# First block, w_o: merged tiles split during the last branch, running sums of the norm behind the last product

## The reference, cut to what matters

```
merged = (gates[:, :, 0] * (y_a @ w_branch[0])
          + gates[:, :, 1] * (y_b @ w_branch[1])
          + gates[:, :, 2] * (y_c @ w_branch[2]))
mix = merged @ w_o
x = layer_norm(ALPHA * x + mix, ln1_g, ln1_b)      # mean and variance over the 1024 features
ffn = conv_ffn(x, w_up, conv_w, conv_b, w_down)
```

## Time and profile before

| | us |
|---|---|
| median of 3 runs | 3969.03 (3965.19 to 3970.46) |
| the profiled execution's own time | 3969.89 |
| its span | 3968.1 |
| PE busy | 3705.0 (93%) |
| DVE busy | 1700.1 (43%) |
| ACT busy | 1516.1 (38%) |
| POOL busy | 1311.7 (33%) |

### The profile page before, as it was taken

The page is one execution under the profiler, slowest core; times in us unless marked ns, Lnnn a source line. Parts: engine busy times, 40 slices in busy tenths (PEclk is TensorE's granted clock), DMA queues, the critical chain, the costliest instruction groups (busy, mean ns, idle before and its releaser), DMA issues.

```text
span 3968.1 us, 47959 instructions
## 1 busy us (share of the span) xinstructions
PE 3705.0 (93%) x17594; PEld 2921.5 (74%) x17594; DVE 1700.1 (43%) x2434; ACT 1516.1 (38%) x2470; POOL 1311.7 (33%) x600
## 2 busy tenths in 40 slices
PE   8989997999898999989998799999899898999998
PEld 7777785888687777768887576888534687777886
DVE  3444346543334433664325642503447443425042
ACT  3246632432322665233324544423243233444232
POOL 4422132444343112334443243344201011443442
PEclk9989998999998999999999899999999999999999
DMA  3211121322222111222332132222123100322222
GB/s 136 98 67 43 43 75 57 102 95 101 88 92 96 43 43 49 90 69 95 101 101 91 64 104 77 85 99 97 65 69 91 33 1 1 101 96 81 100 95 80
DMA packets 100066, 308.85 MB, mean 78 GB/s; under 512 B 25920, under 2 KB 26048, under 8 KB 99520
## 3 DMA queue, kind: packets, MB, share of 16 engines
q1 hardware_dynamic: 81792, 298.90, 22.4%
q10 hardware_dynamic: 18112, 7.68, 0.8%
HBM read 301.30 MB, written 4.19 MB: 77 GB/s over the span
## 4 chain that ended last, share of the span: by engine, by line
issue 45%; PE 35%; POOL 16%; DVE 2%; ACT 1%; DVEq 0%; POOLq 0%; DMA 0%; SPq 0%; ACTq 0%
POOL ring_r L2584 16%; PE ps L437 8%; PE ps L438 8%; PE ps L439 8%; PE ps L915 2%; PE ps L1015 1%; PE ps L934 1%; PE ps L596 1%; PE ps L1083 0%; PE ps L1060 0%; PE ps L1091 0%; PE ps L1073 0%; PE ps L1051 0%; PE ps L1093 0%; PE ps L1153 0%
## 5 line engine op out<-in xcount | busy, mean ns | idle before, releaser
L2584 POOL TENSOR_TENSOR ring_r<-ring,rounded_r 128x1024 fp32r<-128x1024 f32 x520 | 1272.6, 2450 | 2156.7 <-ACT rounded_r L1196 2156.2
L437 PE MATMUL ps<-source_hi,rounded_r 128*128 128x512 f32 x2560 | 1019.7, 398 | 120.4 <-DVE X_lo L1886 30.9
L1196 ACT ACTIVATE rounded_r<-ring 128x1024 fp32r<-128x1024 f32 x520 | 550.4, 1059 | 1383.1 <-PE ps L439 1214.0
L438 PE MATMUL ps<-source_hi,ring_r 128*128 128x512 f32 x2560 | 1007.2, 393 | 0.0
L437 PEld LDWEIGHTS ps<-source_hi,rounded_r 128*128 128x128 f32 x2560 | 487.7, 191 | 238.0 <-DVE N_lo L2181 33.4
L439 PE MATMUL ps<-X_lo,rounded_r 128*128 128x512 f32 x1536 | 602.5, 392 | 0.0
L438 PEld LDWEIGHTS ps<-source_hi,ring_r 128*128 128x128 f32 x2560 | 487.8, 191 | 101.9 <-issue 2.6
L439 PEld LDWEIGHTS ps<-X_lo,rounded_r 128*128 128x128 f32 x1536 | 291.0, 189 | 61.6
L439 PE MATMUL ps<-N_lo,rounded_r 128*128 128x512 f32 x768 | 303.0, 394 | 0.0
L2141 DVE SCALAR_TENSOR_TENSOR T<-ps,PAR,T 128x511 f32<-128x511 f32 (+1 forms) x176 | 131.5, 749 | 229.4 <-ACT T L1384 214.5
L437 PE MATMUL ps<-H_hi,rounded_r 128*128 128x512 f32 x512 | 199.2, 389 | 0.0
(11 more groups left out here) (496 smaller groups left out, 5791.6 us busy)
## 6 DMA issues: line engine op xcount, KB each, us to landing
ring<-in_weights SPq DMA_DIRECT2D x560, 512.0 KB, 3.3
X<-in_x SPq DMA_DIRECT2D x2, 1024.0 KB, 7.0
out_x<-X SPq DMA_DIRECT2D x4, 512.0 KB, 2.6
SWAP<-Z ACTq DMA_DIRECT2D x4, 256.0 KB, 3.3
MEM<-in_mem ACTq DMA_DIRECT2D x1, 1024.0 KB, 4.7
diag_in<-Y ACTq DMA_DIRECT2D x8, 128.0 KB, 2.2
Z<-diag_in ACTq DMA_DIRECT2D x8, 128.0 KB
diag_out<-Z ACTq DMA_DIRECT2D x2, 512.0 KB, 4.4
```

The source lines that it names most:

```text
L437: mm(o, lh, rh, start=start, stop=False)
L438: mm(o, ll, rh, start=False, stop=False)
L1196: av(RH[:, j, :], ring[:, j, :], ACT.Copy).then_inc(w_hi, 1)
L2584: nc.gpsimd.tensor_tensor(RL[:, j, :], ring[:, j, :], RH[:, j, :].bitcast(F32), ALU.subtract).then_inc(w_lo, 1)
```

## The change

Three edits, in the first block of each layer.

* DVE and ACT: the splits of the merged tiles are put between the work on the last branch. ACT makes `MR[0]`, `MR[1]` behind the round of c = 9, `MR[2]`, `MR[3]` behind c = 10, `MR[4]`, `MR[5]` behind c = 11, then rounds the fourth slot, then makes `MR[6]`, `MR[7]`. DVE makes `ML[0]` to `ML[3]` just ahead of the gate multiplies of tiles 4 to 7, and `ML[4]` to `ML[7]` behind tile 7.
* PE: `first_quad` of w_o takes its first nine steps in a skewed order, (lane 0, k 0), (0, 1), (1, 0), (1, 1), (0, 2), (1, 2), (2, 0), (2, 1), (2, 2), and goes on from k = 3 abreast as before. Each lane now also waits until DVE has read its PSUM bank (`mg`).
* PE: `sums` and `sums_of(6)` stand behind the last product, ahead of `sums_of(7)`; nothing stands ahead of it or inside it.

```diff
+            def first_quad(split, bank, hi, lo, ready, base, step=1, banks_free=None, lanes=RING - 1, before=None, skewed=False):
+                def step_of(k, j):
+                    pe.wait_ge(ready, base + step * (k + 1))
+                    if k == 0:
+                        pe.wait_ge(w_lo, split + (j + 1))
+                        if banks_free is not None:
+                            pe.wait_ge(banks_free[0], banks_free[1] + (j + 1))
+                    ins = three(ps[:, bank + j, :], wh(j, k), wl(j, k), tile(hi, k), tile(lo, k), k == 0, k == KT - 1)
+                    if k == KT - 1:
+                        ins.then_inc(used, 1)
+                if skewed:
+                    for j in range(2):
+                        for k in range(2):
+                            step_of(k, j)
+                    for j in range(2):
+                        step_of(2, j)
+                    for k in range(3):
+                        step_of(k, 2)
+                for k in range(3 if skewed else 0, KT):
...
                     for j in range(lanes):
+                        step_of(k, j)
...
-                first_quad(W0 + n_split(B_WO), 0, MR, ML, y_lo, l * Y_N + 12)
+                first_quad(W0 + n_split(B_WO), 0, MR, ML, y_lo, l * Y_N + 12, 1, (mg, l * 24 + 24), skewed=True)
                 shift(l, 0)
                 for j in range(RING):
                     pe.wait_ge(x1pre, l * RING + RING + (j + 1))
-                    if j == RING - 1:
-                        sums(l, 0)
-                    product(W0 + (n_split(B_WO) + RING + j), j, j, MR, ML, (lambda: sums_of(l, 0, KT - 2)) if j == RING - 1 else None)
+                    product(W0 + (n_split(B_WO) + RING + j), j, j, MR, ML)
+                sums(l, 0)
+                sums_of(l, 0, KT - 2)
                 sums_of(l, 0, KT - 1)
...
+                def merged_high(*tiles):
+                    for n in tiles:
+                        act.wait_ge(mg, l * 24 + 4 + 16 + n + 1)
+                        av(MR[n], M[n], ACT.Copy).then_inc(y_hi, 1)
                 for c in range(12):
                     act.wait_ge(used, C + B_BR + c + 1)
                     ahead(Q + (B_BR + c) // RING, c % RING)
-                for n in range(KT):
-                    act.wait_ge(mg, l * 24 + 4 + 16 + n + 1)
-                    av(MR[n], M[n], ACT.Copy).then_inc(y_hi, 1)
+                    if c >= 9:
+                        merged_high(2 * (c - 9), 2 * (c - 9) + 1)
                 last_slot(Q + B_WO // RING)
+                merged_high(6, 7)
...
+                def merged_low(n):
+                    dve.wait_ge(y_hi, l * Y_N + 12 + n + 1)
+                    remainder(ML[n], M[n], MR[n].bitcast(F32), y_lo)
                 for b in range(3):
                     for n in range(KT):
+                        if b == 2 and n >= 4:
+                            merged_low(n - 4)
...
-                for n in range(KT):
-                    dve.wait_ge(y_hi, l * Y_N + 12 + n + 1)
-                    remainder(ML[n], M[n], MR[n].bitcast(F32), y_lo)
+                for n in range(4, KT):
+                    merged_low(n)
```

More of the change, by code:

```diff
@@ L451, in wl @@
                 return RL[:, j, k * P:k * P + P]
-            def first_quad(split, bank, hi, lo, ready, base, step=1, banks_free=None, lanes=RING - 1, before=None):
-                for k in range(KT):
+            def first_quad(split, bank, hi, lo, ready, base, step=1, banks_free=None, lanes=RING - 1, before=None, skewed=False):
[17 more added lines that the diff above has]
+                for k in range(3 if skewed else 0, KT):
                     if before is not None and k == before[0]:
                         before[1]()
-                    pe.wait_ge(ready, base + step * (k + 1))
                     for j in range(lanes):
[L460 to L466, removed]
+                        step_of(k, j)
                 for j in range(lanes, RING):
```

## The result

The changed kernel takes 3941.11 us (median; 3939.27 to 3945.74, 4 runs) against 3969.57 us: the ratio is 0.9932, 95% interval 0.9915 to 0.9949, so 28.5 us less where 25.6 were forecast. The same kernel, run again later beside some of the experiments, gave 3940.27 against 3970.91 us, ratio 0.9915 (0.9902 to 0.9929). The profiled execution has a span of 3943.9 us.

A forecast was written before the change was run, and what follows sets the result against it. PE, busy 93% of the span, was taken as the bound, so only its gaps or slow-clock stretches could give time: 6.1 + 6.7 = 12.8 us per layer, 25.6 for both, giving 3943.4 us; range 3936 to 3953.

The forecast's parts named there:

- The first gap: PE's wait before w_o for the first low part: 7.5 us per layer, 5.1 idle, the rest at half clock.
- Part 1: Splits of the merged tiles during the last branch, so w_o starts without the gap: gain 6.1 us per layer.
- the wait of 0.8 us at k = 3: At the start of w_o, PE waits 0.8 us for `ML[3]`, taken as held by POOL until 603.1.
- The holds: DVE steps reading two on-chip tiles beside a POOL operation end only behind it; `ML[1]` held to 594.9.
- Part 2: Sums moved behind the last w_o product, so the square of tile 7 comes earlier: gain 6.7 us per layer.
- The wait for weights ahead of the last product: At the end of w_o, PE idles 2.0 us until POOL delivers the last chunk's low part.
- The moved sums are hidden: Behind the last product, four moved products (3.4 us) cost nothing; PE has 1.6 us of slack before the mean.
- The sum: Both gains added over the first block: 12.8 us per layer, 25.6 for both layers.
- the one given 0.12: DVE held less than counted at w_o's start, by `ML[3]` in time or halved rates: 3941 to 3942.5; chance 0.12.
- The reading by which contention halves the rates: DVE and POOL each run at half rate when sharing memory: 14.1 us per layer, 3940.8; chance called small.
- The slow tail: Last w_o product runs at 1.2 GHz throughout, moved sums end late: 9.8 us per layer, 3949.4; chance 0.08.
- hold-and-clock rival: POOL holds DVE more, PE waits some 2 us at w_o's start, clock falls: 10.5 per layer, 3948.0; chance 0.08.

The follow-up runs named there:

- the filled gap: Kernel before the change, with 23 matmuls of unused result between the last branch and w_o in each layer; ratio 1.0004 to before.
- the sums alone: Kernel before the change, with only the sums moved behind the last w_o product; 3957.95 us, ratio 0.9965 to before.
- weights early: Changed kernel, with the last w_o chunk rounded ahead of the square of tile 4 instead of behind it; 3944.95 us in one execution.
- more sums: Changed kernel, with four more full-precision matmuls of unused result between the last product and the moved sums; ratio 0.9921 to before.
- unskewed kernel: Changed kernel, with the first nine w_o steps abreast again, lanes 0, 1, 2 for each k; 3955.38 us, ratio 0.996 to before.

## Why the prediction was right

* *The first gap costs 7.5 us, 5.1 idle and the rest clock.* Right. The twelfth w_o matmul now comes 7.5 us earlier (9.98 to 2.49; 7.3 in layer 1), and the filled gap gives 2.1 of them back with w_o starting no earlier.
* *Part 1, 6.1 us per layer.* The mechanism was right, the size low: 7.0 and 6.9 from the border to DVE's first residual (15.66 against 22.69, 15.61 against 22.52). The term that was mis-sized is the wait of 0.8 us at k = 3, which did not come. (The sum also takes off 0.1 for which it names no row.) I had `ML[3]` lose a race of 0.2 us against POOL, with the transfer of the fourth slot read from coarse slices and ACT's round at 3.3 us behind the border. ACT started it at 3.7, POOL at 4.8, and `ML[3]` had begun at 4.2. Lane 2 was expected 0.5 late and starts 0.36 late (603.62 instead of 603.26).
* *The holds.* `ML[1]` was expected to end at 594.9, 4.3 us behind the end of c = 10, and does so (598.27, the round of c = 10 having begun at 593.93); the held steps end 0.54 to 0.56 behind POOL, before and after. The Trainium skill (GPSIMD Engine Reference, "8. Key points") has contention for instructions with two SBUF inputs; the rows agree on which are hit, and show that one waits for the other to end (2.89 against 0.68 us).
* *Part 2, 6.7 us per layer.* 7.2 and 7.1 in the changed kernel, 6.9 with the sums alone. The square of tile 7 comes 1.64 us behind its add (1.7 expected) and the table load is followed at once by JUNK. The last half microsecond lies earlier in DVE's chain: from the first residual to tile 7 it took 33.7 us, and 34.2 were expected from the kernel before, since POOL's three operations beside DVE's first steps came without a pause in the changed kernel and held DVE less (the four operations of the earlier trace rows took 3.93 us and one step before them 2.43, instead of 6.14 and 0.69).
* *The wait for weights ahead of the last product: 2.0.* It is 1.44 and 1.31, and costs nothing (weights early).
* *The moved sums are hidden with 1.6 us to spare.* Right that they are hidden, but the cover is larger: 1.4 up to the mean, and the hold behind it adds 1.7 (more sums).
* *The sum.* 25.6 expected, 28.3 in the stage, 28.5 in the median. Of the cases listed it was not quite the forecast's that came, but the one given 0.12, `ML[3]` in time (3941 to 3942.5). The reading by which contention halves the rates gave 14.1 per layer and 3940.8, the nearest number of all, and that is luck: the steps beside POOL are held to its end (2.89 and 2.57 us), and what made up the difference is `ML[3]` and the half microsecond of DVE's chain. The slow tail did not come: the clock stays at 1.00 over 637 to 645 in spite of the 1.44 us of waiting, and of the hold-and-clock rival only the unskewed kernel shows something, in one layer.

## What to carry to other kernels

Follow the chain that a removed wait uncovers to its second and third step, and price in it the holds between DVE and POOL: here neither weights that came 1.4 us earlier nor four added matmuls moved the end of the norm by half a microsecond. Put the first steps of a product in the order in which their inputs become ready; that was 2.8 to 4.5 of the 7 us that the early splits gave, and nearly nothing without them. A short idle stretch of PE costs more than its length where the clock falls behind it (5.1 us of idleness cost 7.5), but what is saved of that can be lost again in part behind the next gap (2.1 us saved, 1.5 left).

## What the runs showed that I had not expected

* The clock behind a wait of 2.86 us of PE fell in one layer (granted 0.71 over the 4 us from 604) and cost nothing beyond the wait in the other, in one execution of the unskewed kernel.
* A step of DVE that POOL holds is a slack for all that comes before it: 3.4 us of extra PE work cost 0.35.
